# A gated convolution mixer in seven block products for eight, with GpSimd forming low parts in its output product

## What is computed

```python
def short_conv_mixer(x, w_in, conv_w, w_out):          # the odd layer's mixer
    proj = jnp.einsum('bsd,de->bse', x, w_in)          # 1024 -> 3 x 1024
    gate_b, gate_c, h = jnp.split(proj, 3, axis=-1)
    z = gate_c * h
    zp = jnp.pad(z, ((0, 0), (CONV_WIDTH - 1, 0), (0, 0)))
    conv = sum(conv_w[k] * zp[:, k:k + s] for k in range(CONV_WIDTH))   # 3 taps over tokens
    return jnp.einsum('bse,ed->bsd', gate_b * conv, w_out)

x = layer_norm(alpha * x + mix, ...)
hid = square(relu(x @ ffn_w1))                          # 1024 -> 4096
x = layer_norm(alpha * x + hid @ ffn_w2, ...)
x = x + sigmoid(x @ ple_gate_w) * (p[i] @ ple_w)
```

## Time and profile before

| | |
|---|---|
| median of three runs | 2101.3 us |
| profiled execution: span, first to last instruction | 2099.5 us |
| its time outside the span (not listed; median less span) | 1.8 us |
| PE, DVE, ACT, POOL busy | 99%, 59%, 38%, 35% |
| granted TensorE clock, mean | 1.000 |
| moved by DMA | 287 MB, mean 137 GB/s |
| mixer of the odd layer, about | 1000 to 1350 us of the span |
| FFN trips of the odd layer | 1403 to 1670 us |

### The profile page before, as it was taken

How to read it: one execution, slowest core, us unless ns; L and a number is a source line. 1 busy time by engine, 2 the same in 40 slices (tenths; PEclk the granted TensorE clock), 3 DMA queues, 4 the chain that set the end, 5 groups by cost and what they waited for, 6 DMA issues and landing times.

```text
span 2099.5 us, 25079 instructions
## 1 busy us (share of the span) xinstructions
PE 2088.8 (99%) x9605; PEld 1735.1 (83%) x9605; DVE 1237.6 (59%) x1619; ACT 788.2 (38%) x1165; POOL 732.5 (35%) x493
## 2 busy tenths in 40 slices
PE   9999999999999999999999999999999999999999
PEld 9888788888888888888888888888888888888887
DVE  4744775565666657664543352675556566666563
ACT  3112454544543334531211101455444544334530
POOL 5113167778502000221422322268777512000220
PEclk9999999999999999999999999999999999999999
DMA  5111124344599555311121111124434599554221
GB/s 187 41 61 52 30 81 155 140 147 162 179 360 390 192 199 172 111 41 30 41 81 41 58 44 45 36 81 155 156 136 160 184 376 377 193 189 170 96 86 40
DMA packets 180819, 287.17 MB, mean 137 GB/s; under 512 B 12800, under 2 KB 71260, under 8 KB 180700
## 3 DMA queue, kind: packets, MB, share of 16 engines
q1 hardware_dynamic: 180000, 285.26, 39.6%
q10 hardware_dynamic: 700, 0.31, 0.1%
HBM read 221.56 MB, written 63.96 MB: 136 GB/s over the span
## 4 chain that ended last, share of the span: by engine, by line
PE 94%; POOL 2%; DVE 2%; issue 1%; ACT 1%; ACTq 0%; POOLq 0%; DVEq 0%
PE bank_a L1851 17%; PE bank_a L1853 17%; PE bank_a L1852 17%; PE bank_b L1851 14%; PE bank_b L1853 14%; PE bank_b L1852 14%; POOL op_lo L1021 1%; PE bank_a L1890 1%; PE bank_b L1890 1%; POOL op_sum L1094 1%; DVE xt_lo L1393 1%; DVE xt_hi L1388 0%; ACT op_hi L1249 0%; PE bank_a L2069 0%; PE bank_a L2078 0%
## 5 line engine op out<-in xcount | busy, mean ns | idle before, releaser
L1007 POOL TENSOR_TENSOR w_lo<-raw,w_hi 128x512 fp32r<-128x512 f32 x148 | 207.8, 1436 | 861.3 <-ACT w_hi L1115 861.2
L1851 PE MATMUL bank_a<-xt_hi,w_hi 128*128 128x512 f32 x640 | 251.4, 393 | 0.1
L1853 PE MATMUL bank_a<-xt_hi,w_lo 128*128 128x512 f32 x640 | 249.2, 389 | 0.0
L1852 PE MATMUL bank_a<-xt_lo,w_hi 128*128 128x512 f32 x640 | 249.1, 389 | 0.0
L1219 ACT CAST hop_hi<-h_raw 128x1024 fp32r<-128x1024 f32 x112 | 117.8, 1051 | 243.6 <-PE bank_a L1853 145.1
L1592 DVE TENSOR_TENSOR hop_lo<-h_raw,hop_hi 128x1024 fp32r<-128x1024 f32 x112 | 137.5, 1227 | 118.1 <-ACT hop_hi L1219 117.9
L1853 PE MATMUL bank_a<-wop_hi,hop_lo 128*128 128x512 f32 x512 | 199.2, 389 | 0.0
L1851 PE MATMUL bank_a<-wop_hi,hop_hi 128*128 128x512 f32 x512 | 199.2, 389 | 0.0
L1852 PE MATMUL bank_a<-wop_lo,hop_hi 128*128 128x512 f32 x512 | 199.2, 389 | 0.0
L1115 ACT CAST w_hi<-raw 128x512 fp32r<-128x512 f32 x148 | 82.4, 621 | 284.7 <-PE bank_a L1853 154.7
L1021 POOL TENSOR_TENSOR op_lo<-op_sum,op_hi 128x512 fp32r<-128x512 f32 x112 | 165.7, 1497 | 11.1 <-ACT op_hi L1249 6.7
(11 more groups left out here) (198 smaller groups left out, 4741.2 us busy)
## 6 DMA issues: line engine op xcount, KB each, us to landing
w_raw<-in_ffn_w_dram SPq DMA_DIRECT2D x144, 512.0 KB, 6.3
h_raw<-h_spill SPq DMA_DIRECT2D x112, 512.0 KB, 5.4
h_spill<-h_tile SPq DMA_DIRECT2D x170, 256.0 KB, 2.3
w_raw<-in_ffn_w_dram SPq DMA_DIRECT2D x112, 256.0 KB, 3.4
raw<-in_od_w_in_dram SPq DMA_DIRECT2D x48, 256.0 KB, 2.8
raw<-in_ple_gate_w_dram SPq DMA_DIRECT2D x32, 256.0 KB, 3.6
h_spill<-h_tile2t SPq DMA_DIRECT2D x28, 256.0 KB, 2.0
raw<-in_ev_w_in_dram SPq DMA_DIRECT2D x24, 256.0 KB, 3.2
```

The source lines that it names most:

```text
L1007: pool.tensor_tensor(lo, raw[:, n % NRAW, :], hi.bitcast(F32), ALU.subtract).then_inc(lo_split, 1)
L1851: pe.matmul(dst, s_hi, m_hi, start=first, stop=False, skip_group_check=on_top)
L1852: pe.matmul(dst, s_hi, m_lo, start=False, stop=False, skip_group_check=on_top)
L1853: return pe.matmul(dst, s_lo, m_hi, start=False, stop=last, skip_group_check=on_top)
```

## The change

The mixer takes the FFN's form. Block 0's `c` and `h` stay plain, the other ten blocks (b of block 0, then c, h and b of blocks 1 to 3) become trips of seven products, `bgate` and the block-wise `out` go, and the output product becomes 14 items of 24 matmuls, for two pairs of blocks, at the end, in the order m1 0, m2 0, m1 1, m2 1, then m6, m5, m3, m7 and m4 for pair 0 and pair 1. In the items POOL forms `hop_lo`, with its own semaphore, and DVE only `wop_lo`. In the last trip S3 stands before S4. The classes `Ahead` and `Trips`, `wsum`, `prep`, `prod` and `step` are made general over the layer with base counts; the FFN's own instructions and their order stay.

The order, in the plan:

```diff
+    def short_conv():
+        add("c", slab=("od", D), half=0, paced=True, split_next=True, inner=[turn])
+        add("tsum", layer=OD).unit = turn.unit
+        add("c", half=1, paced=True, last=True)
+        add("thi", layer=OD, half=1)
+        for i in (-4, -3, -2):
+            trip_step(OD, i)
+        add("thi", layer=OD, half=3)
+        add("h", slab=("od", 2 * D), half=1, load_next=False, split_next=False)
+        add("t4", layer=OD)
+        add("thi", layer=OD, half=2)
+        trip_step(OD, -1)
+        add("h", half=0, last=True)
+        for i, (b, op) in enumerate(tr.seq):
+            trip_step(OD, i)
+            if i == 1:
+                add("thi", layer=OD, half=4)
+            if op == "S2" and PLAIN < b <= PLAIN + TT:
+                add("alpha", tiles=[b - PLAIN - 1])
+            if b == last and op in ("S3", "S4"):
+                prepare(OD, ("S3", "S4").index(op))
+        for i, (form, j) in enumerate(OD_ITEMS):
+            while nxt < len(OD_ITEMS) and (a.user_before(nxt) is None or a.user_before(nxt) < i):
+                prepare(OD, nxt)
+                nxt += 1
+            st = add("prod", item=i, layer=OD, head=form_heads.get(form))
...
+            if OD_ITEMS[i] == ("m3", OD_PAIRS - 1):
+                squares_of(lo)
+                add("stats", half=0, ln=2)
+                add("norm", half=0, ln=2)
+            if OD_ITEMS[i] == ("m4", 0):
+                turns("ln", 0, [0, 1, 2, 3], ln=2)
+        squares_of(hi)
+        add("stats", half=1, ln=2)
+        turns("ln", 0, [4, 5, 6, 7], ln=2, ring="B")
+        add("norm", half=1, ln=2)
+        add("split", layer=OD)
-    for blk in range(OD_BLOCKS):
-        if blk == 0:
-            feature_halves("c", ("od", D), "gate")
...
-        block_out(("od_out", blk * BLK), ln=2 if blk == OD_BLOCKS - 1 else None)
+OD_SLOTS = (0, 1, 2, 3, 4, 0, 1, 2, 3, 4, 0, 2, 1, 3)
```

The evictions of a trip by DVE. Per kind of block and product the steps are:

```diff
+OD_STEPS = dict(
+    c=dict(S1=("s15",), A22=("c21",), S2=("u1",), A12=(), S4=("c12",), S3=("c22",)),
+    h=dict(S1=("s15",), A22=("c21", "m21", "v100", "v101", "v102", "v110", "v111", "v112"), S2=("u1",), A12=("m11",),
+           S4=("c12", "m12", "v000", "v001", "v002", "v010", "v011", "v012"), S3=("c22", "m22")),
+    b=dict(S1=("s15",), A22=("c21", "g21", "h4"), S2=("u1",), A12=("g11",), S4=("c12", "g12"),
+           S3=("c22", "g22", "h1", "h2", "h3")))
+OD_LAST = dict(OD_STEPS["b"], S3=("c22", "g22"), S4=("c12", "g12", "h1", "h2", "h3"))
...
+                if op == "S4":
+                    dve.wait_ge(trip_done, tr.done[b, op])
+                    od_wait(b, "u1")
+                    dve.tensor_tensor(q12, q12, bank, ALU.add).then_inc(od_step, 1)
+                    if kind == "h":
+                        od_wait(b, "c12")
+                        dve.tensor_tensor(q12, q12, cv_12[:, :], ALU.mult).then_inc(od_step, 1)
+                        od_wait(b, "m12")
+                        od_conv(b, blk, 0, 0)
+                        od_conv(b, blk, 0, 1)
```

s15, u1, c12, c22 and c21 are additions that read a bank (S1's, S2's, then the same banks again after S4, S3 and A22); m and g are products with the gate; v are the taps of a convolution, three operations each (`od_conv`, as L1792 to L1795 before); h1 to h4 are sums. A plain `h` of block 0 has its two products for each half, and all twelve tap operations behind those of half 0. An item's low parts:

```diff
+                if st.kind == "prep" and st.layer == OD:
+                    a, i = ahead[OD], st.item
+                    k = a.slot(i)
+                    pool.wait_ge(ahead_hi, a.act[i] - 1)
+                    pool.tensor_tensor(hop_lo[k][:, :, :], h_raw[a.hop_chunk(i)][:, :, :],
+                                       hop_hi[k][:, :, :].bitcast(F32), ALU.subtract).then_inc(od_hop_low, 1)
...
-                    dve.wait_ge(ahead_hi, a.act[i] - 1)
-                    dve.tensor_tensor(hop_lo[k][:, :, :], h_raw[a.hop_chunk(i)][:, :, :],
-                                      hop_hi[k][:, :, :].bitcast(F32), ALU.subtract).then_inc(ahead_dve, 1)
+                    if st.layer != OD:
+                        dve.wait_ge(ahead_hi, a.act[i] - 1)
+                        dve.tensor_tensor(hop_lo[k][:, :, :], h_raw[a.hop_chunk(i)][:, :, :],
+                                          hop_hi[k][:, :, :].bitcast(F32), ALU.subtract).then_inc(ahead_dve, 1)
...
+                    if a.low_by_pool:
+                        pe.wait_ge(od_hop_low, a.hop_low[i])
```

SP's part at the end of the trips (`load_od_item` waits for the spill of its role, for its hop buffer to be free on `od_hop_low`, and for its weight buffer to be free on `ahead_dve`; item 7's weight buffer is item 3's):

```diff
+                if kind == "b":
+                    if op == "A12":
+                        spill_g(b, 0, "g11", cv_11)
+                    if op == "S3":
+                        spill_g(b, 3, "g22", cv_22)
+                    if op == ("S4" if b == last else "S3"):
+                        for role, name, tile in ((4, "h1", b_12), (5, "h2", b_22), (2, "h3", cv_12)):
+                            spill_g(b, role, name, tile)
+                    if op == "A22":
+                        spill_g(b, 1, "g21", cv_21[blk % 2])
+                        spill_g(b, 6, "h4", b_21)
+                if (b, op) == (last, "A11"):
+                    load_od_item(0)
+                if (b, op) == (last - 1, "A22"):
+                    load_od_item(1)
+                if (b, op) == (last, "A12"):
+                    load_od_item(2)
+                if (b, op) == (last, "S4"):
+                    load_od_item(4)
+                if (b, op) == (last, "A22"):
+                    for n in (3, 5, 6):
+                        load_od_item(n)
```

More of the change, by code:

```diff
@@ L163, in pair @@
[L163 to L170, removed]
+                taken += items[i][1] < pairs - 1 and not (joined and i == n - 2)
+                self.taken.append(taken)
+        self.total = dict(act=base["act"] + 2 * n, dve=dve, taken=taken, pool=base["pool"] + pairs,
+                          hop=base["hop"] + n, load=base["load"] + loads)
     def user_before(self, i):
@@ new lines, in w_user, with w_before, pair, slot @@
+    def w_user(self, load):
+        i = max(i for i in range(len(self.items)) if self.first_load[i] <= load)
+        if self.items[i][0] == "m6":
+            return self.sum[i]
+        return self.dve[i]
+    def w_before(self, load):
+        return next((k for k in range(load - 1, -1, -1) if self.w_chunk(k) == self.w_chunk(load)), None)
+class FfnAhead(Ahead):
+    def pair(self, i):
+        return (self.items[i][1] + 1) % PAIRS
+    def slot(self, i):
+        return i % 5 if i < LAST_FORM else LAST_SLOTS[i - LAST_FORM]
+    def hop_chunk(self, i):
+        return (192, 196, 48, 52, 128, 132, 200)[i % 7] if i < LAST_FORM else (192, 196, 200)[(i - LAST_FORM) % 3]
@@ new lines, in first_read, with make_trips, make_ahead @@
+    def first_read(self, b, op):
+        name = {"S4": "s15", "S3": "u1", "A22": "c22"}[op]
+        return ("odstep", self.step[b, name]) if self.layer == OD else ("hid", self.hid[b, name])
+def make_trips():
+    trips, before = {}, None
+    for layer, end in ((0, FFN_BLOCKS), (OD, PLAIN + len(OD_TRIPS)), (1, FFN_BLOCKS)):
+        trips[layer] = before = Trips(layer, before, end)
+    return trips
+def make_ahead():
+    first = FfnAhead(0, None, ITEMS, PAIRS, True)
+    mixer = OdAhead(OD, first, OD_ITEMS, OD_PAIRS, False, True)
+    return {0: first, OD: mixer, 1: FfnAhead(1, mixer, ITEMS, PAIRS, True)}
@@ L260, in make_plan @@
     held = {"A": [None] * RING, "B": [None] * RING}
-    trips = [Trips(layer) for layer in range(2)]
-    ahead = [Ahead(layer) for layer in range(2)]
+    trips, ahead = make_trips(), make_ahead()
     need = dict(xu=[0, 0], hu=[0, 0])
@@ L1214, in stage @@
                     else:
[L1216 removed]
+                        tr = trips[st.layer]
+                        act.wait_ge(trip_done, tr.done[tr.end - 1, ("S1", "S2", "A12", "S4", "A22")[i]])
                     slot, landed = a.hop_landed(i)
```

581 lines of the change are left out of this document (410 added, 171 removed).

## The result

The changed kernel takes 2130.0 us (median of 4 runs, 2126.7 to 2131.4) where the kernel before takes 2101.3 in the same comparison: 1.0135 of its time, 95% interval 1.012 to 1.0149. That is 29 us slower. The profiled execution took 2129.25 us, with a span of 2127.5. The forecast was 2099.6, in a range of 2084 to 2114.

A forecast was written before the change was run, and what follows sets the result against it. PE's matmul count was taken as the bound, with nothing hidden behind a wait. Waits of 36.4 us against 38.1 saved gave -1.7, so 2097.8 of span and 2099.6 us, in a range of 2084 to 2114.

The forecast's parts named there:

- 168 matmuls: Mixer: matmuls fall from 1536 to 1368, at 0.227 us each 38.1 us less if PE never waits.
- h trips: Blocks 1 and 2: DVE's convolution burst makes A22, the next S3 and the next S1 wait, 4.4 us per trip.
- contended progress of 0.42: h trips: beside POOL, DVE's convolution steps progress at 2.07/4.9 = 0.42 of their speed alone.
- Block 3 and last trip: With S3 before S4, A22 waits 0.5 us, S2's low part 3.7 and S3 0.8: 5.0 us.
- Start: First mixer trips: DVE's queue delays reads; S4 waits 5.8 us, S3 1.6, next S1 0.8: 8.2 us.
- Where both engines have work, a DVE operation takes about one POOL operation's time: Durations used throughout: beside POOL, three convolution steps on DVE take about 4.9 us instead of 2.07.
- Output: Output product: steady state costs nothing, but filling makes item 3 wait 2 us, m6 8 and m5 1: 11 us.
- Rival C: m1's flush at T0+34 (T0: last trip's end) or later, output 16 us, h trips' upper ends: 2112 us; chance 0.14.
- Tail: End of output product: the last four turns wait for m4's flushes, about 1 us.
- Handovers: Some twelve stalls each cost 0.2 us from the release to the matmul: 2.4 us.
- Rival E: TensorE's clock falls after three long pauses, 2.7 us each, 8 us on top of the sum: 2108 us; chance 0.10.
- a PSUM reader is spared: Durations used: a DVE operation that reads PSUM keeps its 0.69 us with POOL running beside it.

The follow-up runs named there:

- e5: Changed kernel, with DVE starting its sums ahead of the mixer's trips only after GpSimd's four low parts of the plain h block's weights: 2125.5 us.
- e6: Changed kernel, with DVE instead of GpSimd forming the low parts of the gated operand in the output product: 2117.0 us, ratio 1.0076.
- e18: e17 with the low parts of the output product's gated operand on GpSimd again instead of DVE: 2099.1 us, ratio 0.9989.
- e7: Changed kernel, with the statistics and normalisation of token half 0 behind the flush of m7 instead of ahead of it: 2122.7 us.
- e3: Changed kernel, with PE filling four of its waits with transposes of the identity into a free bank: 2127.1 us.
- e17: e12 with item 4's weights loaded before item 3, m6's flush ahead of item 10's weight sum, and each convolution's first step on ACT: 2085.6 us.
- e8: Changed kernel, with DVE's flush of m1 ahead of item 5's weight sum, where DVE was idle: 2131.1 us.
- e10: e5 with the plain h block's twelve convolution steps put between the reads of the first trip: 2124.0 us.
- e13: e12 with at most six convolution steps ahead of each read of a bank in the trips: 2106.0 us.
- e4: Changed kernel, with half 0's six convolution steps behind DVE's read of S3's bank in the h trips of blocks 1 and 2: 2124.2 us.
- e12: Changed kernel with e4, e5, e6, e8, e10, S4 before S3 in the last trip, block 3's convolutions moved, item 3 served first: 2102.6 us.

## Why the prediction was wrong

The miss is 29.7 us of span (forecast -1.7, measured +28.0): 10.5 of waits and 19.2 beside them, of which 17.6 are slow matmuls. With its waits alone the kernel would take 2110 us, inside the range; the clock, which the sum put at nothing, took it out.

- *168 matmuls, 38.1 us.* Right.
- *h trips, 8.8 with the next S1.* Right: A22 3.1 and 3.1, S1 1.0 and 0.8, 8.0 in all. The contended progress of 0.42, from the earlier trace rows, gave 3.2 for A22's 3.1.
- *Block 3 and last trip, 5.0.* Right: A22 0.3, S2 3.4, S3 1.2; 4.9.
- *Start, 8.2.* It is 11.5: the plain h block waits 6.4, and since PE comes so much later, S4 only 1.9 instead of 5.8; S3 1.3, S1 1.9. The step that failed is the one not there: POOL's low parts for this block, with DVE's new sums beside them. "Where both engines have work, a DVE operation takes about one POOL operation's time" does not hold here: DVE's sums keep their 1.2 us and POOL's four take 15.96, which e5 puts down to those sums.
- *Output, 11.* It is 16.5: item 3 5.2 for 2, m6 11.3 for 8. Rival C's condition was met, "DVE's six operations and POOL's three serialise", at 3.3 to 3.4 us each for four of the six. Item 3's load was late for the reason given, but by more: the spill it needs was issued at 1280.6, behind item 4's 2 MB, and the load went at 1287.4, 6.8 us later where the sum had 2.3. The sentence that failed is "in steady state POOL's 3.4 fits in 5.44 and the move costs nothing": POOL's time fits, but DVE pays 2.1 us for each meeting (e6, e18: 13 us).
- *Tail, 1.* The wait it named, of the last turns, is 0.2. Another of 3.8 came that no term held: m4 waits for m7's flush, which stands on DVE behind the statistics and ACT's root; the clock behind it is 0.66, and e7 took back 7.3 us.
- *Handovers, 2.4.* 2.2 is left for them.
- *The clock.* Rival E had the mechanism and a chance of 0.10, as three falls of 2.7 us; there were eight stretches of 1.3 to 2.9 us, 2.2 on average and 17.6 together. It was kept out of the sum though the sum itself held the pauses that cause it: E's 2.7 us on each of the five waits over 3 us that the sum held is 13.5, and the forecast 2113. Seven of the eight stretches lie behind a measured wait over 3 us; the one at 1080 us lies behind shorter ones, which no rival had.

E and the output part of C (2 + 11 + 3 = 16, measured 16.5) came true at the same time, and the forecast treated them as alternatives. C's upper ends for the h trips and the last trip did not come.

One reading of the prediction is not in its row. DVE's operation on PSUM at 1046.89 was nearly over when POOL began at 1047.53, so its 0.69 us does not show that a PSUM reader is spared. The one at 1052.54 in the same trace does (L1803, 0.69 us), for POOL's row lasts until 1053.66.

## What to carry to other kernels

When a saving on PE is paid for with waits, add what the clock takes behind the pauses: here 46.9 us of gaps came with 17.6 of slow matmuls, in eight stretches. Keeping PE busy in the pauses gave back little (e3, 2.8 us); taking the waits away gave back more (e6, e7). Before you move an operation from DVE to POOL while both have SBUF work in the same stretch, price the meetings (13 us here, twice); look for work that ACT can take instead (e17: 16 steps moved, 13.8 us). And when a wait at one place goes without the time following (e8, e10, e13), the named flush was only where a full engine was met: unload that engine.

## What the runs showed of the hardware

- POOL can be shut out far longer than one operation: 12.3 us for one of 1.3, while DVE ran its row at the full 1.2 us for each sum. In the earlier trace rows and in the filling the two take turns. What decides between the two stays open. It is not that DVE's operations stand without a wait: in the filling too each starts 0.08 us before the one ahead of it ends (1302.78, 1306.12). By the Trainium skill ("SBUF — State Buffer", section "Who interferes with whom") the port pair that DVE and GpSimd share is held for a whole instruction and the other side blocks: that agrees with DVE's 3.3 to 3.4 beside POOL's 2.4, but would let POOL in after each DVE instruction, and the one that began at 1014.66 was not let in.
- The clock fell behind pauses of 3.1 us, and also behind one of 1.8: in e4 the first S4 waits 1.8 us until 1068.0, and from 1069.2 on matmuls start every 0.43 us. The same wait in the changed kernel, 1.9 us, left it at 1.00. It does not always fall at once: behind A22's 3.1 us the next matmul took 0.79 in e6's first h trip and 0.50 in its second, and the 10 us around each have 0.83. Nor does it fall behind every longer pause: behind item 4's 3.5 us in e17 the windows show 1.00 and 0.98, behind m5's 3.3 us 0.85. By the Trainium skill ("TensorE: Matmul & The Clock Gate", section "What's actually happening") the array's clock is halved once it has been idle; the trace agrees in that starts go from 0.227 to 0.43 us apart behind a pause, though not behind each.
- The transfers of the filling ran at 380 to 393 GB/s for 30 us (e12, e17, e18). Item 4 still waits 3.5 us in e17, for its weights' chain of transfer, POOL, DVE and ACT; whether fewer bytes there would take that away stays open, it was not tried.
